# Expert products of an MoE layer in three single-pass parts instead of one float32 product, with the parts made by ScalarE and VectorE

## The chip, the cores and the metric

The kernel runs on one core of a Trainium2 chip. The metric is the device time of one execution in microseconds. The kernel before took 673.37 us, the median of three runs (673.04 to 673.84).

## The reference

One layer of a decoder trunk for 1024 prompt tokens and 64 sample tokens (1088 in all) with 1024 channels: RMSNorm, one input projection to 2048 columns for four token mixers, an output projection with residual, then RMSNorm and a mixture of experts (a group of 8 experts is chosen first, then the best two in it), residual, final RMSNorm. The change touches the experts:

```python
hg = jnp.einsum('nd,edf->nef', xt, w_gate.astype(x.dtype))   # 32 experts, d = 1024, f = 128
hu = jnp.einsum('nd,edf->nef', xt, w_up.astype(x.dtype))
act = jax.nn.silu(hg) * hu * gates[:, :, None]
out = jnp.einsum('nef,efd->nd', act, w_down.astype(x.dtype))
```

Only the two chosen experts of a token have a gate that isn't zero, so the kernel gathers for each expert the rows of its tokens.

## The kernel before

Every engine has its own hand-written program and they meet at semaphores, so the order of the work on an engine is the order of the code. After the projections (up to about 376 us of the span) comes routing: counts, places and a table of the tokens of each expert. Then come the expert blocks. A block is up to 128 rows of one expert; there are 32 blocks, n = 0 to 31, one for each expert, and behind them as many overflow blocks as experts have more than 128 rows. In this run there are three, n = 32 to 34 (35 blocks in all).

For block n the engines do this:

- POOL (GpSimd) issues **gather n**, an indirect DMA of the rows of the normed tokens from DRAM into one of four slots of `xg` (L1047), and later **scatter n**, an indirect DMA of the block's result to DRAM (L1062). In its program gather n+3 stands ahead of scatter n-1. Before the first gather POOL zeroes all four slots with one memset (L1070).
- PE: **T(n)**, 8 transposes of the gathered rows into PSUM (L1918). **GU(n)**, gate and up at once: 8 float32 matmuls with 256 moving columns, of which each shows as two records in the trace (L1932, "x16"). **AT(n)**, one transpose (L1941). **D(n)**, the down projection, 2 float32 matmuls of 512 columns, 4 records (L1952).
- ACT: `hTm`, the copy of T(n) out of PSUM (L862), silu (L869), the copy of AT(n) (L877), half of the output (L886).
- DVE: the product of silu and up, `actv` (L1542), the other half of the output, `outb` (L1550).

The order on PE is T(n+1), AT(n-1), GU(n), D(n-1), and then the same for the next n. Ahead of the blocks DVE computes how many overflow blocks there are (L1515 to L1533).

SP loads the weights of a block: gate, up and down, 512 KB each, 1.57 MB in all (L506). Eight sets fit in SBUF (`wfirst` holds three, `wlater` five), so the load for block n starts once D(n-8) has ended. The loads are held back by a second rule: the up part for block n isn't issued before all three parts of block n-1 have landed:

```python
if m == 1 and not (first and j <= FIRST):
    sp.wait_ge(w_in_sem[(j - AHEAD) % LAP], 48 * (lap(i, j - AHEAD) + 1))
```

So the time at which the up part for n+1 is issued tells when the weights of block n had landed; this time is called **L(n)** below.

The rest of the kernel already works with split values elsewhere: the input projection (L1663, L1709) and the output projection (L1840) take each float32 factor as a high part (a copy rounded to the type float32r, by ACT, L606) and a low part (the difference, by DVE, L1150), and sum three products high·high, high·low, low·high, each one pass through PE.

Of the kernel before, what the change touches and what calls it, by code (L numbers as in the profile page):

```python
# [19 lines left out]
F32 = mybir.dt.float32  # L20
# [96 lines left out]
def build_layer(nc, a):  # L117
    with ExitStack() as ctx:
# [15 lines left out]
        o_end = o_uc + 2 * CL * 4  # L134
# [17 lines left out]

        xg = at("xg", [P, XG, D], o_xg)
# [7 lines left out]
        def opair(i):  # L161
# [44 lines left out]
        otmp = at("otmp", [1, OVER, NE], o_w + 8192)  # L206
        otmp2 = at("otmp2", [1, OVER, NE], o_w + 10240)
# [6 lines left out]
        wsT = sb("wsT", [P, NG, P])  # L214
        wsb = sb("wsb", [NS, NG, NS])
        pw = sb("pw", [P, 2, P])
# [71 lines left out]
            "xt_done", "htm_ready", "gu_done", "sg_ready", "act_ready", "at_done", "att_ready",  # L288
# [285 lines left out]
        def _(act):  # L574
# [280 lines left out]
            def expert_hT(i, j):  # L855
# [6 lines left out]
                nc.scalar.activation(hTm[:, j % 2, :, :], src, ACT.Copy).then_inc(s["htm_ready"], 1)  # L862
# [26 lines left out]
            def step(i, j, first, last):  # L889
                if not last:  # L890
                    expert_hT(i, j + 1)
                else:
                    with act.If(total > 0):
                        expert_hT(i, j + 1)
# [7 lines left out]
            act.wait_ge(s["o_done"], TILES)  # L902
            expert_hT(0, 0)
# [12 lines left out]
            with act.Fori(0, OVER // LAP) as i:  # L916
                with act.If(i * LAP < total):
                    for j in range(LAP):
                        with act.If(i * LAP + j < total):
                            with act.If(i * LAP + j + 1 < total):  # L920
                                expert_hT(i + NE // LAP, j + 1)
                            expert_actT(i + NE // LAP, j - 1)
                            expert_silu(i + NE // LAP, j)
                            expert_out(i + NE // LAP, j - 1)
# [26 lines left out]
        def _(pool):  # L951
# [117 lines left out]
            pool.wait_ge(s["o_done"], TILES)  # L1069
            do(g.memset(xg[:].rearrange("p s d -> p (s d)"), 0.0), s["xg_zero"])  # L1070
# [13 lines left out]
            for b in range(-3, NE + 1):  # L1084
                if b == 0:
                    pool.wait_ge(s["idx_ready"], 2)
                if b + 3 < NE:
                    c = (b + 3) * CAPB
                    gather(b + 3, gidxs[:, c:c + 1], tab[:, c:c + 1], b if b >= 1 else None)
                else:  # L1090
                    if b + 3 == NE:
# [3 lines left out]
                    gather_over(b + 3 - NE)  # L1095
# [9 lines left out]
            def over_from(o):  # L1105
# [3 lines left out]
                with pool.If(total > o):  # L1109
                    if o + 4 < OVER:  # L1110
                        gather_over(o + 4)
# [12 lines left out]
        def _(dve):  # L1124
# [389 lines left out]
            n_e, incl = ov[:, 0, :], ov[:, 1, :]  # L1514
            do(ts(ovi[:], carry[0:1, :], float(P - 1), None, ALU.add))  # L1515
            do(ts(ovi[:], ovi[:], 7, None, ALU.logical_shift_right))
            do(ts(n_e, ovi[:], 1.0, -1.0, ALU.max, ALU.add))
            do(v.tensor_tensor_scan(incl, ones[0:1, 0:NE], n_e, 0.0, ALU.mult, ALU.add))
            grid = [1, OVER, NE]
            for k in range(2):  # L1520
                dve.wait_ge(h2_stored[k], 16 * ((TILES + 1 - k) // 2))
            do(tt(otmp[:], incl.unsqueeze(1).broadcast_to(grid), iob[:].unsqueeze(2).broadcast_to(grid),
                  ALU.is_le))
            do(v.tensor_reduce(ovb[:, 0, :], otmp[:], AX_X, ALU.add))
            do(tt(otmp2[:], otmp[:], n_e.unsqueeze(1).broadcast_to(grid), ALU.mult))
            do(v.tensor_reduce(ovb[:, 1, :], otmp2[:], AX_X, ALU.add))
            do(ts(ovb[:, 0, :], ovb[:, 0, :], float(NE - 1), None, ALU.min))
# [500 lines left out]
```

## Time and profile before

| | |
|---|---|
| median of the runs | 673.37 us (673.04 to 673.84) |
| profiled execution, its own time | 673.23 us |
| its span, first to last instruction | 671.4 us |
| busy in the span: PE, DVE, ACT, POOL | 580.5, 369.5, 204.3, 97.6 us |
| moved by DMA | 116.27 MB, mean 173 GB/s |

The profiled execution's own time is 1.83 us more than its span; that is what lies around the span. PE's busy time counts overlapping records and waits inside them, so it says that PE was always occupied, not that it ran at its peak. The expert blocks take about 399 to 617 us of the span. After them come the pairing of the results, the residual and the last norm, which use no PE.

### The profile page before, as it was taken

The numbers are of one execution on the slowest core, as the hardware profiler recorded it, in microseconds if no ns is written. First come the engines' busy times: TensorE is split into PE (matmuls) and PEld (weight loads), VectorE is DVE, ScalarE is ACT, GpSimd is POOL, SyncE is SP. The second block draws the span as 40 slices with busy tenths as digits, with TensorE's granted clock in tenths as the row PEclk, the third lists the DMA queues.
The fourth block names the chain that finished last, engine by engine and source line by source line (L and its number), as shares of the span: only waits on it lengthen the run. The fifth ranks groups of instructions, "written<-read, shape, count | busy, mean of one in ns | idle before, by whom it ended". The sixth has DMA issues, their size and how long they took to land. (4 is left out here: it accounts for less than half of the span.)

```text
span 671.4 us, 9514 instructions
## 1 busy us (share of the span) xinstructions
PE 580.5 (86%) x3131; PEld 496.4 (74%) x3131; DVE 369.5 (55%) x653; ACT 204.3 (30%) x351; POOL 97.6 (15%) x151
## 2 busy tenths in 40 slices
PE   3899999999999998999999449999999999997000
PEld 2899999988898897888887338777778777774000
DVE  4838997999996966566665841111111111112497
ACT  6732112311324273122121123233333323332132
POOL 4300002000000000000000231332233333322000
PEclk9999999999999999999999759999999999999555
DMA  9660211120122123641220776888989999940784
GB/s 320 133 143 1 63 32 32 53 63 16 48 72 95 33 94 138 238 157 64 95 79 32 255 241 218 297 307 285 317 294 351 367 316 344 322 186 26 288 349 161
DMA packets 51439, 116.27 MB, mean 173 GB/s; under 512 B 8434, under 2 KB 26743, under 8 KB 50295
## 3 DMA queue, kind: packets, MB, share of 16 engines
q1 hardware_dynamic: 42899, 92.82, 40.7%
q0 software_dynamic: 6656, 17.84, 7.6%
q10 hardware_dynamic: 1828, 4.96, 2.0%
q8 instruction: 25, 0.41, 0.3%
q14 instruction: 31, 0.25, 0.1%
HBM read 99.75 MB, written 20.68 MB: 179 GB/s over the span
## 5 line engine op out<-in xcount | busy, mean ns | idle before, releaser
L1663 PE MATMUL ps<-at_hT,at_ring 128*128 128x384 f32 x936 | 165.7, 333 | 1.1 <-ACT at_wk L629 1.1
L1663 PEld LDWEIGHTS ps<-at_hT,at_ring 128*128 128x128 f32 x936 | 155.8, 188 | 6.5 <-issue 5.0
L1840 PE MATMUL ps<-at_hT,at_mring 128*128 128x512 f32 (+1 forms) x432 | 102.6, 393 | 1.9 <-DVE at_mring L1343 1.2
L1840 PEld LDWEIGHTS ps<-at_hT,at_mring 128*128 128x128 f32 (+1 forms) x432 | 77.3, 182 | 21.2 <-DVE at_mring L1343 1.6
L1542 DVE TENSOR_TENSOR at_actv<-at_sg,ps 128x128 f32<-128x128 f32 x35 | 10.1, 287 | 146.2 <-ACT at_sg L869 101.6
L1190 DVE SCALAR_TENSOR_TENSOR at_mixP<-at_uc,sb_par,at_mixP 128x1024 f32<-128x1024 f32 x60 | 77.4, 1289 | 2.1
L1932 PE MATMUL ps<-at_wlater,at_hTm 128*128 128x256 f32 x320 | 72.4, 379 | 0.0
L1932 PEld LDWEIGHTS ps<-at_wlater,at_hTm 128*128 128x128 f32 x320 | 59.2, 190 | 7.2
L1932 PE MATMUL ps<-at_wfirst,at_hTm 128*128 128x256 f32 x240 | 56.3, 389 | 0.0
L1918 PEld LDWEIGHTS ps<-sb_ident,at_xg 128*128 128x128 f32 x280 | 37.7, 193 | 23.6 <-issue 21.8
L1932 PEld LDWEIGHTS ps<-at_wfirst,at_hTm 128*128 128x128 f32 x240 | 45.9, 197 | 6.3 <-issue 0.3
L1550 DVE COPY at_outb<-ps 128x512 f32<-128x512 f32 x35 | 24.2, 692 | 41.5 <-PE ps L1952 41.5
L1062 POOL DMA_INDIRECT scratch_out<-at_outb,at_tab x32 | 30.4, 950 | 102.3 <-DVE at_outb L1550 98.8
L1918 PE MATMUL ps<-sb_ident,at_xg 128*128 128x128 f32 x280 | 38.7, 283 | 7.4 <-DMA at_xg<-scratch_h,at_gidxs 6.2
L581 ACT ACTIVATE at_wk<-at_x 128x1024 f32<-128x1024 f32 (+1 forms) x18 | 19.0, 1058 | 79.9 <-DVE at_x L1415 52.4
L862 ACT ACTIVATE at_hTm<-ps 128x1024 f32<-128x1024 f32 x35 | 35.8, 1024 | 15.7 <-PE ps L1918 15.4
L1619 PE MATMUL ps<-sb_ident,at_wk 128*128 128x128 f32 (+1 forms) x144 | 23.6, 319 | 17.6 <-DVE at_wk L1133 13.9
L1047 POOL DMA_INDIRECT at_xg<-scratch_h,at_gidxs x32 | 31.7, 991 | 47.7 <-issue 36.7
L1952 PE MATMUL ps<-at_wlater,at_actT 128*128 128x512 f32 x80 | 37.6, 592 | 0.0
L886 ACT ACTIVATE at_outb<-ps 128x512 f32<-128x512 f32 x35 | 20.9, 597 | 52.0 <-PE ps L1952 52.0
L1619 PEld LDWEIGHTS ps<-sb_ident,at_wk 128*128 128x128 f32 (+1 forms) x144 | 21.2, 200 | 20.3 <-issue 13.1
L869 ACT ACTIVATE at_sg<-ps 128x128 f32<-128x128 f32 x35 | 9.7, 278 | 84.0 <-PE ps L1932 79.2
(238 smaller groups left out, 656.4 us busy)
## 6 DMA issues: line engine op xcount, KB each, us to landing
at_wlater<-in_expert_w_gate SPq DMA_DIRECT2D x20, 512.0 KB
at_wlater<-in_expert_w_up SPq DMA_DIRECT2D x20, 512.0 KB
at_wlater<-in_expert_w_down SPq DMA_DIRECT2D x20, 512.0 KB
at_raw<-in_w_in SPq DMA_DIRECT2D x16, 512.0 KB, 4.0
at_opair_p<-scratch_out SPq DMA_DIRECT2D x8, 1024.0 KB, 12.0
at_wfirst<-in_expert_w_gate SPq DMA_DIRECT2D x15, 512.0 KB
at_wfirst<-in_expert_w_up SPq DMA_DIRECT2D x15, 512.0 KB
at_wfirst<-in_expert_w_down SPq DMA_DIRECT2D x15, 512.0 KB
```

What stands on the lines that cost most here:

```text
L862: nc.scalar.activation(hTm[:, j % 2, :, :], src, ACT.Copy).then_inc(s["htm_ready"], 1)
L886: nc.scalar.activation(outb[:, j % 2, 0:512], ps[:, 5, :], ACT.Copy)\
L1047: g.indirect_dma_start(xg[0:n, b % XG, :], None, hs, bass.IndirectOffsetOnAxis(ap=index[0:n, :], axis=0), bounds_check=last_token, oob_is_ ...
L1062: g.indirect_dma_start(orow, bass.IndirectOffsetOnAxis(ap=index[0:n, :], axis=0), outb[0:n, b % 2, :], None, bounds_check=last_pair, oob_i ...
L1190: do(stt(y, x, par[:, c, k:k + 1], y, ALU.mult, ALU.add))
L1550: v.tensor_copy(outb[:, j % 2, 512:D], ps[:, 6, :]).then_inc(s["ob_dve"], 1)
L1619: mm = pe.transpose(ps[:, banks + k // 4, k % 4 * P:k % 4 * P + n], wk[0:n, i % 2, 0:D].rearrange("p (q k) -> p k q", k=KC)[:, k, :], iden ...
L1663: mm = pe.matmul(ps[:, bank + r, 0:t1 - t0], w[:, wpart, k * P:(k + 1) * P], hT[:, hpart, k, t0:t1], start=(m, wpart, hpart) == (0, 0, 0), ...
L1840: mm = pe.matmul(ps[0:n, b + r, :], mring[:, 1 - i % 2, mpart, k * P:k * P + n], wo[:, wpart, k, r * 512:(r + 1) * 512], start=(c, mpart, ...
L1918: mm = pe.transpose(ps[:, k // 4, k % 4 * P:(k % 4 + 1) * P], xg[:, j % XG, :].rearrange("p (q k) -> p k q", k=KC)[:, k, :], ident[:])
L1932: mm = pe.matmul(ps[:, 2 + j % 2, 0:2 * FF].rearrange("p (g f) -> p g f", g=2), hTm[:, j % 2, k, :], w[:, :, k, :], start=k == 0, stop=k = ...
L1952: mm = pe.matmul(ps[:, 5 + r, :], actT[:, j % 2, :], wexp(j)[:, q:q + 512], start=True, stop=True)
```

## The change

There are four parts.

1. GU(n) is no longer 8 float32 matmuls but 24 float32r matmuls: high·high, high·low, low·high for each of 8 chunks. The low part of the tokens (`hTm_lo`, L1587 of the changed kernel) is made by DVE from PSUM and `hTm`. The high part of the weights (`whi`, 2 halves, one buffer each, so that the half for n+1 is written once GU(n) has read it) is made by ACT, and the low part (`wlo`) by DVE, which overwrites the landed weights.
2. POOL's order: gather n+4 stands ahead of scatter n-1, where it was gather n+3.
3. The overflow counts on DVE are moved behind the first conversions and cut in two pieces.
4. The four slots of `xg` are zeroed by four ACT copies (three behind the last `square`, one behind the last `h2T` copy) and not by POOL.

Some small arrays also move to other addresses (`wsT`, `wsb`, `pw`), which share room with `hTm_lo`. The core of the diff:

```diff
+        whi = [at("whi0", [P, 2, KC // 2, FF], o_raw + D * 2, F32R),
+               at("whi1", [P, 2, KC // 2, FF], o_sg + D * 4, F32R)]
...
-        hTm = at("hTm", [P, 2, KC, P], o_hTm)
+        hTm = at("hTm", [P, 2, KC, P], o_hTm, F32R)
+        hTm_lo = [at("hTm_lo0", [P, KC, P], o_w + 2 * D * 4, F32R),
+                  at("hTm_lo1", [P, KC, P], o_late, F32R)]
...
+                if i >= LAST:
+
+                    act.wait_ge(s["o_done"], TILES)
+                    for n in range(3) if i == LAST else range(3, XG):
+                        zeros = ones[:].unsqueeze(1).broadcast_to([P, KC, P])
+                        do(A(xg[:, n, :].rearrange("p (k t) -> p k t", k=KC), zeros, ACT.Copy, scale=0.0),
+                           s["xg_zero"])
...
+            def expert_whi(i, j, h):
+
+                b = i * LAP + j
+                act.wait_ge(w_in_sem[j % LAP], 48 * lap(i, j) + 48)
+                if not (isinstance(b, int) and b < 1):
+                    act.wait_ge(s["gu_done" if h else "gu_half"], b)
+                nc.scalar.activation(whi[h][:], half(wexp(j), h), ACT.Copy).then_inc(s[f"w_hi{h}"], 1)
...
             def step(i, j, first, last):
+                ahead(i, j, last, expert_hT)
                 if not first:
                     expert_actT(i, j - 1)
+                ahead(i, j, last, whi0)
                 expert_silu(i, j)
+                ahead(i, j, last, whi1)
                 if not first:
                     expert_out(i, j - 1)
 
 
             act.wait_ge(s["o_done"], TILES)
+            whi1(0, 0)
+            act.wait_ge(s["idx_ready"], 2)
+            whi0(0, 0)
             expert_hT(0, 0)
...
-            pool.wait_ge(s["o_done"], TILES)
-            do(g.memset(xg[:].rearrange("p s d -> p (s d)"), 0.0), s["xg_zero"])
+            pool.wait_ge(s["xg_zero"], XG)
...
-            def step(i, j, first):
+            def expert_hT_lo(i, j):
+
+                b = i * LAP + j
+                dve.wait_ge(s["htm_hi"], b + 1)
+                if not (isinstance(b, int) and b < 2):
+                    dve.wait_ge(s["gu_done"], b - 1)
+                src = ps[:, 0:2, :].rearrange("p b (k t) -> p (b k) t", t=P)
+                v.tensor_tensor(hTm_lo[j % 2][:], src, hTm[:, j % 2, :, :].bitcast(F32),
+                                ALU.subtract).then_inc(s["htm_lo"], 1)
+
+            def expert_wlo(i, j, h):
+
+                b = i * LAP + j
+                dve.wait_ge(s[f"w_hi{h}"], b + 1)
+                v.tensor_tensor(half(wexp_lo(j), h), half(wexp(j), h), whi[h][:].bitcast(F32),
+                                ALU.subtract).then_inc(s[f"w_lo{h}"], 1)
...
+            def step(i, j, first, last):
+                ahead(i, j, last, expert_hT_lo)
+                ahead(i, j, last, wlo0)
                 expert_act(i, j)
+                ahead(i, j, last, wlo1)
                 if not first:
                     expert_out(i, j - 1)
 
...
+            wlo1(0, 0)
+            wlo0(0, 0)
+            expert_hT_lo(0, 0)
+            overflow_counts()
+            expert_hT_lo(0, 1)
+            overflow_blocks()
+            wlo0(0, 1)
+            expert_act(0, 0)
+            wlo1(0, 1)
...
                 if not early(b, 1):
-                    pe.wait_ge(s["htm_ready"], b)
+                    pe.wait_ge(s["htm_lo"], b)
...
-                pe.wait_ge(s["htm_ready"], b + 1)
+                pe.wait_ge(s["htm_lo"], b + 1)
                 if not early(b, 2):
                     pe.wait_ge(s["act_ready"], b - 1)
-                pe.wait_ge(w_in_sem[j % LAP], 48 * lap(i, j) + 48)
-                w = wexp(j)[:, 0:2 * D].rearrange("p (g k f) -> p g k f", g=2, k=KC)
+                out = ps[:, 2 + j % 2, 0:2 * FF].rearrange("p (g f) -> p g f", g=2)
                 for k in range(KC):
-                    mm = pe.matmul(ps[:, 2 + j % 2, 0:2 * FF].rearrange("p (g f) -> p g f", g=2),
-                                   hTm[:, j % 2, k, :], w[:, :, k, :], start=k == 0, stop=k == KC - 1)
-                mm.then_inc(s["gu_done"], 1)
+                    h = k // 4
+                    if k % 4 == 0:
+                        pe.wait_ge(s[f"w_lo{h}"], b + 1)
+                    high, low = whi[h][:, :, k % 4, :], half(wexp_lo(j), h)[:, :, k % 4, :]
+                    x, x_low = hTm[:, j % 2, k, :], hTm_lo[j % 2][:, k, :]
+                    pe.matmul(out, x, high, start=k == 0, stop=False)
+                    pe.matmul(out, x, low, start=False, stop=False)
+                    mm = pe.matmul(out, x_low, high, start=False, stop=k == KC - 1)
+                    if k % 4 == 3:
+                        mm.then_inc(s["gu_done" if h else "gu_half"], 1)
```

On PE, this is the program of the kernel before around GU(1): the transposes T(2), AT(0), GU(1), D(0).

```order
738 L1918 MATMUL ps<-sb_ident,at_xg 128x128 x8
739 L1941 MATMUL ps<-sb_ident,at_actv 128x128
740 L1932 MATMUL ps<-at_wfirst,at_hTm 128x256 x8
741 L1952 MATMUL ps<-at_wfirst,at_actT 128x512 x2
742 L1918 MATMUL ps<-sb_ident,at_xg 128x128 x8
```

In the changed kernel the same place reads as follows (`at_whi_54` is the first half of the high weights, `at_wfirst_lo` the low part in place of the landed weights, `at_hTm_lo_61` the low part of the tokens of block 1).

```order
761 L2024 MATMUL ps<-sb_ident,at_xg 128x128 x8
762 L2053 MATMUL ps<-sb_ident,at_actv 128x128
763 L2042 MATMUL ps<-at_whi_54,at_hTm 128x256
764 L2043 MATMUL ps<-at_wfirst_lo,at_hTm 128x256
765 L2044 MATMUL ps<-at_whi_54,at_hTm_lo_61 128x256
766 L2042 MATMUL ps<-at_whi_54,at_hTm 128x256
767 L2043 MATMUL ps<-at_wfirst_lo,at_hTm 128x256
768 L2044 MATMUL ps<-at_whi_54,at_hTm_lo_61 128x256
```

One row of 8 matmuls has become 24 rows of one, in threes; the order of T, AT, GU, D is the same.

On DVE, this is the end of the overflow counts and the first blocks before (`at_ovt` is the table of overflow blocks).

```order
408 L1532 CAST at_ovt<-at_ovb 1x16
409 L1533 CAST at_ovt<-at_ov 1x1
410 L1542 TENSOR_TENSOR at_actv<-at_sg,ps 128x128 x2
411 L1550 COPY at_outb<-ps 128x512
412 L1542 TENSOR_TENSOR at_actv<-at_sg,ps 128x128
413 L1550 COPY at_outb<-ps 128x512
```

And this is it in the changed kernel, from the last row of the overflow table to the end of the step of block 2 (`at_whi_54` and `at_whi_55` are the two halves).

```order
413 L1644 CAST at_ovt<-at_ov 1x1
414 L1594 TENSOR_TENSOR at_wfirst_lo<-at_wfirst,at_whi_54 128x2x512
415 L1570 TENSOR_TENSOR at_actv<-at_sg,ps 128x128
416 L1594 TENSOR_TENSOR at_wfirst_lo<-at_wfirst,at_whi_55 128x2x512
417 L1587 TENSOR_TENSOR at_hTm_lo_60<-ps,at_hTm 128x1024
418 L1594 TENSOR_TENSOR at_wfirst_lo<-at_wfirst,at_whi_54 128x2x512
419 L1570 TENSOR_TENSOR at_actv<-at_sg,ps 128x128
420 L1594 TENSOR_TENSOR at_wfirst_lo<-at_wfirst,at_whi_55 128x2x512
421 L1578 COPY at_outb<-ps 128x512
422 L1587 TENSOR_TENSOR at_hTm_lo_61<-ps,at_hTm 128x1024
```

Three subtractions of 1024 columns stand around the two instructions that DVE had in a block, and `actv`, for which PE waits, stands behind two of them. On ACT the step changes in the same way. Before, for block 1 and its neighbours:

```order
153 L862 ACTIVATE at_hTm<-ps 128x1024
154 L877 ACTIVATE at_actT<-ps 128x128
155 L869 ACTIVATE at_sg<-ps 128x128
156 L886 ACTIVATE at_outb<-ps 128x512
157 L862 ACTIVATE at_hTm<-ps 128x1024
```

And in the changed kernel:

```order
159 L885 ACTIVATE at_hTm<-ps 128x1024
160 L908 ACTIVATE at_actT<-ps 128x128
161 L893 ACTIVATE at_whi_54<-at_wfirst 128x1024
162 L900 ACTIVATE at_sg<-ps 128x128
163 L893 ACTIVATE at_whi_55<-at_wfirst 128x1024
164 L917 ACTIVATE at_outb<-ps 128x512
165 L885 ACTIVATE at_hTm<-ps 128x1024
```

Silu now stands behind the first half of the next block's weights, and the output half behind the second.

## Rows read from the trace of the kernel before

**Rows 1.** The page: span and instructions.

```profile
span 671.4 us, 9514 instructions
```

**Rows 2.** The chain of work that ended last: start us, us, what.

```profile
389.98 4.42 DMA at_xg<-scratch_h,at_gidxs
...
394.54 1.96 PE ps L1918 x8
...
399.64 5.45 PE ps L1932 x16
...
406.18 3.46 PE ps L1932 x16
...
412.35 3.46 PE ps L1932 x16
...
609.00 3.46 PE ps L1932 x16
...
617.31 0.70 DVE at_outb L1550
```

**Rows 3.** Groups by form, 0 to 400 us: busy us, mean ns of one.

```profile
L1709 PE MATMUL ps<-at_ring,at_hT 128*128 128x256 f32 x192 | 23.2, 283 | 0.0
```

**Rows 4.** Instructions of a line or tile: ns min/median/max, first and last start.

```profile
L1150 DVE TENSOR_TENSOR at_ring<-at_raw,at_ring x16: 1224/1225/1227, 20.5 to 220.0; 128x1024 fp32r<-128x1024 f32 x16
L606 ACT ACTIVATE at_ring<-at_raw x16: 1058/1062/1066, 14.6 to 212.9; 128x1024 fp32r<-128x1024 f32 x16
L1140 DVE TENSOR_TENSOR at_hT<-ps,at_hT x9: 692/1224/1225, 13.5 to 35.4; 128x1024 fp32r<-128x1024 f32 x8, 128x512 fp32r<-128x512 f32 x1
```

**Rows 5.** Groups by form, 400 to 620 us.

```profile
L862 ACT ACTIVATE at_hTm<-ps 128x1024 f32<-128x1024 f32 x34 | 34.8, 1024 | 11.4 <-PE ps L1918 11.1 <-issue 0.3
L1062 POOL DMA_INDIRECT scratch_out<-at_outb,at_tab x32 | 30.4, 950 | 102.3 <-DVE at_outb L1550 98.8 <-issue 3.5
...
L1047 POOL DMA_INDIRECT at_xg<-scratch_h,at_gidxs x28 | 27.3, 975 | 33.4 <-issue 33.4
L1550 DVE COPY at_outb<-ps 128x512 f32<-128x512 f32 x35 | 24.2, 692 | 41.5 <-PE ps L1952 41.5
...
L1542 DVE TENSOR_TENSOR at_actv<-at_sg,ps 128x128 f32<-128x128 f32 x35 | 10.1, 287 | 146.2 <-ACT at_sg L869 101.6 <-issue 44.6
```

**Rows 6.** The timeline between projection and first block: start us, us.

```profile
375.43 3.52 POOL L1070 MEMSET at_xg<- 128x4096 f32 x1 [0.20 <-POOL sb_rs L963]
...
377.90 0.60 ACT L833 ACTIVATE at_h2T<-ps 128x512 f32<-128x512 f32 x1 [3.63 <-issue]
...
390.35 0.20 DVE L1512 TENSOR_TENSOR sb_stage<-sb_stage 128x36 f32<-128x36 f32 x1
...
395.98 0.14 DVE L1533 CAST at_ovt<-at_ov 1x1 int32<-1x1 f32 x1
```

**Rows 7.** What SP's queue waited for, 400 to 600 us, and two of its issues.

```profile
SPq L506 <- DMA at_wlater<-in_expert_w_down: 68.2, 14, 7.0
SPq L506 <- DMA at_wfirst<-in_expert_w_down: 46.5, 11, 7.3
...
419.54 0.33 SPq L506 DMA_DIRECT2D at_wfirst<-in_expert_w_up  x1
...
588.60 0.33 SPq L506 DMA_DIRECT2D at_wfirst<-in_expert_w_up  x1
```

**Rows 8.** Stretches: busy us by engine, granted clock, DMA share, GB/s.

```profile
400.00:405.00 5.00, 5.00 (x17) 4.06 (x16) 0.00 (x0) 1.99 (x2) 0.05 (x1) 0.64 0.97 251
411.54:593.50 181.96, 181.96 (x860) 141.90 (x859) 28.94 (x59) 61.58 (x119) 56.77 (x63) 1.00 0.91 318
499.90:505.32 5.42, 5.42 (x27) 4.15 (x26) 0.98 (x2) 1.33 (x3) 1.41 (x2) 1.00 0.82 287
518.25:526.02 7.77, 7.77 (x38) 6.22 (x37) 0.98 (x2) 2.22 (x5) 2.51 (x3) 1.00 1.03 394
593.00:594.00 1.00, 1.00 (x6) 0.88 (x5) 0.00 (x0) 0.00 (x0) 0.82 (x1) 1.00 0.17 62
```

More of the change, by code:

```diff
@@ L887, in expert_out, with ahead, whi0, whi1 @@
                     .then_inc(s["ob_act"], 1)
-            def step(i, j, first, last):
+            def ahead(i, j, last, work_on):
                 if not last:
-                    expert_hT(i, j + 1)
+                    work_on(i, j + 1)
                 else:
                     with act.If(total > 0):
-                        expert_hT(i, j + 1)
+                        work_on(i, j + 1)
+            def whi0(i, j):
+                expert_whi(i, j, 0)
+            def whi1(i, j):
+                expert_whi(i, j, 1)
+            def step(i, j, first, last):
+                ahead(i, j, last, expert_hT)
                 if not first:
                     expert_actT(i, j - 1)
+                ahead(i, j, last, whi0)
                 expert_silu(i, j)
+                ahead(i, j, last, whi1)
                 if not first:
@@ L922, in _ @@
                             expert_actT(i + NE // LAP, j - 1)
+                            with act.If(i * LAP + j + 1 < total):
+                                whi0(i + NE // LAP, j + 1)
                             expert_silu(i + NE // LAP, j)
+                            with act.If(i * LAP + j + 1 < total):
+                                whi1(i + NE // LAP, j + 1)
                             expert_out(i + NE // LAP, j - 1)
@@ new lines, in expert_wlo, with ahead @@
+            def expert_wlo(i, j, h):
[3 more added lines that the diff above has]
+                                ALU.subtract).then_inc(s[f"w_lo{h}"], 1)
+            def ahead(i, j, last, work_on):
+                if not last:
+                    work_on(i, j + 1)
+                else:
+                    with dve.If(total > 0):
+                        work_on(i, j + 1)
@@ L1553, in step, with wlo0, wlo1 @@
+            def wlo0(i, j):
+                expert_wlo(i, j, 0)
+            def wlo1(i, j):
+                expert_wlo(i, j, 1)
+            def step(i, j, first, last):
+                ahead(i, j, last, expert_hT_lo)
+                ahead(i, j, last, wlo0)
                 expert_act(i, j)
+                ahead(i, j, last, wlo1)
                 if not first:
                     expert_out(i, j - 1)
-            for j in range(LAP):
-                step(0, j, first=j == 0)
-            with dve.Fori(1, NE // LAP) as i:
-                for j in range(LAP):
-                    step(i, j, first=False)
@@ new lines, in _ @@
+            wlo1(0, 0)
[7 more added lines that the diff above has]
+            wlo1(0, 1)
+            for j in range(1, LAP):
+                step(0, j, first=False, last=False)
+            with dve.Fori(1, NE // LAP - 1) as i:
+                for j in range(LAP):
+                    step(i, j, first=False, last=False)
+            total = dve.value_load(ovt[0:1, 2 * OVER:2 * OVER + 1], min_val=0, max_val=OVER)
@@ L1563, in _ @@
+            for j in range(LAP):
+                step(NE // LAP - 1, j, first=False, last=j == LAP - 1)
             with dve.If(total < 1):
```

92 lines of the change are left out of this document (53 added, 39 removed).

## The prediction

> **What bounds the kernel now.** I read the chain of work that ended last first. From the first gather's landing to the end of the last block it is PE work in program order, with a steady step: GU(1) begins at 406.18, GU(2) at 412.35, GU(34) at 609.00, which is 6.17 us a block, of which GU takes 3.46, and the last output is copied at 617.31 [rows 2]. So in this stretch a microsecond off PE's program is a microsecond off the end, for as long as nothing else is late. What else could be late is seen next, in SP's waits: SP waits 68.2 + 46.5 us, 25 times, for weights that have to land before it may issue the next ones [rows 7]. L(8) is 419.54 and L(33) 588.60 [rows 7], 25 loads in 169.06 us, 6.76 us a load. The loads are thus already slower than the blocks, and it isn't seen only because eight sets of weights fit: the lead is being eaten. The stretches show it from the side of the DMA engines: 0.91 share and 318 GB/s over 182 us, 57.9 MB [rows 8]. The reader should see that PE is the bound now and that the DMA side has a small reserve at the end: L(34) is about 594 (the share falls to 0.17 at 593 [rows 8]; I add 1 us until the semaphore), and GU(34) begins at 609.00, 15 us later.
>
> **GU in three products.** The trace has this very form in another place: 192 matmuls of 256 columns on float32r, high·high, high·low, low·high, in 23.2 us, 0.121 us each [rows 3]. 24 of them are 2.90 us where GU took 3.46 [rows 2], 0.56 us less a block and 5.61 us a block instead of 6.17. From GU(1) to GU(34) that is 33 x 0.56 = 18.5 us, and 0.56 more in GU(34) itself: 19.0 us less. The price from below is the width alone (24 x 256 columns at 2.4 GHz, 2.56 us, another 11 us less); from above it is what GU takes now. I take the row, since the order of the operands is the same.
>
> **The conversions in a block.** DVE gets three subtractions of 1024 columns, 1.225 us each, from SBUF or PSUM alike [rows 4], beside `actv` 0.287 and `outb` 0.692 [rows 5]: 4.65 us of 5.61. ACT gets two copies of 1.062 [rows 4] beside `hTm` 1.024 [rows 5] and small ones. Both fit, but the order counts, so I step through a block with GU(n) beginning at 0. It is half done at 1.45: `whi0` for n+1 until 2.5, `wlo0` until 3.8. GU(n) ends at 2.9: silu, then `whi1` until 4.3, `wlo1` until 5.6. `actv` comes behind `wlo0`, at 4.1, and AT(n) needs it at 5.5. GU(n+1) begins at 5.61 and needs `wlo0` (3.8) then and `wlo1` (5.6) at 7.05. T(n+2) ends at 5.5, `hTm` follows until 6.6 and its low part until 7.9, a whole step ahead of GU(n+2). Nothing stands in PE's way, with 1.4 us to spare. The cost is nothing while this reserve holds.
>
> **The start.** T(0) begins at 394.54 and ends 1.96 later [rows 2]. T(1) now waits for the low part of T(0) too, 1.22 us, and GU(0) begins at about 400.9 and not at 399.64. It runs mostly at the lower clock level: the granted clock was 0.64 between 400 and 405, thus 1.2 GHz for most of it [rows 8], and the old GU(0) took 5.45 [rows 2]. 24 matmuls, most at 256 columns by 1.2 GHz, give about 4.6, until 405.5. DVE is later: the overflow counts took from about 390.8 (two small instructions begin at 390.35) to 396.1 [rows 6], 5.3 us, and now stand between the low parts of blocks 0 and 1, so that the second piece ends at about 406, `wlo0` of block 1 at 407.3 and `actv` of block 0 at 407.6. AT(0) waits for it, and GU(1) begins at 407.7, not at 406.18: 1.5 us more.
>
> **Zeros on ACT, gathers sooner.** The memset lasted 3.52 us on POOL, from 375.43 to 378.95 [rows 6], and POOL's next work, the first gather, came at 389.98 [rows 2], so removing it gives nothing. Three copies on ACT (at most 1.06 each) end at about 377.7, and the `h2T` copy behind them began at 377.90 [rows 6]: nothing to 0.5 us. That gather n+4 passes scatter n-1 moves no gather that PE waits for: after block 1 PE waits for no gather in the chain [rows 2]. It gives a block of lead more.
>
> If only these terms counted, the end would come 19.0 - 1.5 = 17.5 us sooner.
>
> **What is late next: the weights.** The bytes don't change, the time for them does. With D(0) about 0.8 us later (412.3), the load for block 8 starts so much later, and SP goes from load to load by landings as now, so that L(34) moves from 594 to 594.8. The gathers and scatters of the same stretch run on the same engines: 57.9 MB less 27 loads of 1.573 MB leaves 15.4 MB for about 29.5 blocks, 0.52 MB each [rows 8]. At L(34) the changed kernel will be some 2.3 blocks further, 1.2 MB more in the same time. What a megabyte beside a load costs I take from two loads: 5.42 us at 287 GB/s and 7.77 us at 394 GB/s [rows 8], 1.51 MB more in 2.35 us, 1.6 us per MB. From below it is nothing (share 0.91, so there are gaps), from above 1 MB at the mean 318 GB/s, 3.1 us. So L(34) = 594.8 + 1.9 = 596.7, between 594 and 599. Without waits GU(34) would begin at 609.00 - 18.5 + 1.5 = 592.0, and needs the weights some 2.8 us before. It waits: from L(34) on, `whi0` 1.06, `wlo0` 1.23, `actv` of the block before 0.29, AT 0.11 and gaps between engines make 2.9 us. GU(34) = 599.6, which is 9.4 sooner than 609.00; its own 0.56 makes 10.0. The waits begin at block 28 or so, and take back 7.5 of the 17.5 us.
>
> The Trainium skill, DMA: Bandwidth & Descriptors, section Where 436 GB/s comes from, puts the limit of transfers between HBM and SBUF at about 358 GB/s a core. By that the 57.9 MB need 162 us, not 182, the weights would be in time and the whole 17.5 us would stay. The trace has a load at 394 GB/s, above it, and a mean of 318, below it [rows 8]; I go by the landings.
>
> **The sum.** 673.23 us of the profiled execution (671.4 of span [rows 1] and 1.83 around it) less 10.0 is 663.2; the median of the runs is 0.14 higher: 663.4 us. What comes after block 34 isn't touched.
>
> **Rivals.**
> - *A, the weights take over at about block 28* (above): 663.4, with its bounds 660.5 to 666. For it speak the 25 waits of SP on landings. Chance 0.57.
> - *B, DMA keeps up*: the gaps at 0.91 share take the extra traffic and the loads themselves go faster when the engines are never left waiting. PE sets the step to the end: 673.4 - 17.5 = 655.9, 654 to 660. Against it: the rule that holds the up part back for the landing leaves gaps that more traffic doesn't shorten. The rule on 358 GB/s above would end here. Chance 0.18.
> - *C, DVE becomes the bound, slower than before*: POOL issues two indirect DMAs a block, 0.95 and 0.975 us [rows 5]. If DVE's subtractions with two SBUF operands stood still for them, DVE would need 4.65 + 1.92 = 6.57 us a block, 0.40 more than PE needs now: 33 x 0.40 + 1.5 = 14.7 us more, 688. It decides from 1.5 us of standstill a block on. For it: only 0.96 us of DVE's step are free. Against: `sb_stage` at 390.35, with two operands in SBUF, ran in 0.20 us [rows 6] while POOL was issuing the gather of 389.98 [rows 2]. Chance 0.08, with other ways to be slower.
> - *D, the loads are hit harder*: each megabyte at 3.1 us, and the wait of ACT for weights ahead of silu delays also the outputs and scatters: 666 to 671. Chance 0.14.
> - *E, it does nothing to the time*, gain and waits equal: 0.03.
>
> The Trainium skill, SBUF — State Buffer, section Who interferes with whom, says that a VectorE instruction with two SBUF inputs contends with a GpSimd instruction that reads SBUF. This is the mechanism of C. The small instruction at 390.35 doesn't show it; no long one beside a gather is in this trace.
>
> **Numbers.** The likeliest is A, 663.4. A and B and the nearer part of D hold 8 in 10: 655 to 668.5. A measurement of this kernel can tell some 0.2% (1.3 us) from no change. Faster 0.88, same 0.03, slower 0.09.
>
> **What would show it.** In the changed profile: the matmuls of GU at 0.121 us each and 5.6 us a block on PE between 420 and 540; GU(1) at 407 to 408; from about 560 on PE idle 1 us a block, with `whi` waiting for the weights' DMA; SP waiting for landings as before and the last up part issued at about 591; DVE's subtractions at 1.225 us. The prediction is wrong if PE never waits after 420 (B), if the subtractions show 1.7 us or more beside POOL's issues (C), or if a load takes over 7 us in the mean (D).

## The result and the profile after

The changed kernel takes **667.98 us** (three runs, 659.28 to 667.98), against 673.37 us before (five runs, 672.87 to 674.35): ratio 0.9876, 95% interval 0.9844 to 0.9908. Of its five runs two are left out of these ranges and the ratio, one of 843.35 us at a mean granted clock of 0.677 (the others had 0.937 to 0.942), and one of 669.70 us, which is no slower than the slowest of the six further runs below. It gained 5.4 us where 10.0 were forecast. The profiled execution took 667.98 us, with a span of 666.1 us, 1.88 us around it.

The chain of work that ended last, columns as in [rows 2], from the first gather to the end of the blocks:

```profile
390.71 4.47 DMA at_xg<-scratch_h,at_gidxs
...
395.31 1.96 PE ps L2024 x8
...
406.67 1.23 DVE at_wfirst_lo L1594
407.89 0.21 DVE at_actv L1570
408.15 0.33 PE ps L2053
...
414.12 6.86 DMA at_wfirst<-in_expert_w_down
...
594.00 7.33 DMA at_wfirst<-in_expert_w_down
...
601.43 1.07 ACT at_whi L893
...
603.68 0.27 DVE at_actv L1570
603.99 0.33 PE ps L2053
604.32 0.22 PE ps L2042
```

In [rows 2] this stretch was PE from beginning to end. Now it leaves PE behind D(0): from 414.12 on it is the landings of weights, each of which releases the next issue on SP, and it returns to PE only at the last block. The end is that of the forecast: landing, `whi`, `actv`, AT(33), GU(34) at 604.32 (599.6 forecast). From the last landing (601.38) to GU(34) it took 2.94 us, 2.9 were forecast.

What SP and ACT waited for (us in total, times, longest), in the order of [rows 7]:

```profile
SPq L522 <- DMA at_wlater<-in_expert_w_down: 88.5, 16, 7.9
SPq L522 <- DMA at_wfirst<-in_expert_w_down: 45.4, 11, 6.2
...
ACT at_whi L893 <- DMA at_wlater<-in_expert_w_down: 17.9, 6, 5.2
ACT at_whi L893 <- DMA at_wfirst<-in_expert_w_down: 11.5, 6, 3.8
```

SP waits for landings as before. New is that ACT waits too: 12 times the weights weren't there when `whi` wanted them. The stretches, columns as in [rows 8]:

```profile
412.96:520.00 107.04, 107.04 (x723) 88.80 (x723) 86.46 (x98) 78.96 (x117) 42.46 (x38) 1.00 0.91 307
420.99:593.56 172.57, 162.82 (x1078) 133.60 (x1077) 128.33 (x146) 115.17 (x174) 66.80 (x63) 1.00 0.92 314
530.00:540.00 10.00, 7.55 (x52) 6.46 (x53) 6.79 (x10) 5.56 (x10) 1.97 (x2) 1.00 0.99 315
560.00:570.00 10.00, 6.91 (x48) 5.71 (x47) 5.20 (x6) 3.74 (x6) 2.48 (x3) 1.00 0.86 295
```

Until 520 PE has no idle time. Between 530 and 540 and between 560 and 570 it is idle for 2.5 and 3.1 us in ten. The second row is from L(8) to L(33): 25 loads in 172.57 us, 6.90 each (6.76 before, [rows 7]), at 314 GB/s, about the rate of [rows 8]. In this execution more work per microsecond did not make the transfers faster.

### The profile page after: what moved, and what is told of

Read it like the earlier page. It is cut to its first block, busy times and chain, and to the rows that moved or that the text cites. A ratio compares the mean times of both kernels' runs of the same rounds, so it can differ in the third digit from the quotient of the medians.

```text
span 666.1 us, 10376 instructions
## 1 busy us (share of the span) xinstructions
PE 561.1 (84%) x3411; PEld 490.0 (74%) x3411; DVE 487.6 (73%) x758; ACT 275.6 (41%) x425; POOL 105.5 (16%) x150
## 4 chain that ended last, share of the span: by engine, by line
PE 29%; DMA 28%; DVE 18%; ACT 3%; issue 2%; SPq 2%; POOL 0%; DVEq 0%; POOLq 0%; ACTq 0%
DMA at_wlater<-in_expert_w_down 15%; PE ps L1946 13%; DMA at_wfirst<-in_expert_w_down 11%; PE ps L1769 8%; DVE at_x L1697 4%; PE ps L1987 2%; DVE at_mixP L1240 2%; DVE at_x L1705 2%; SPq L522 2%; DVE at_hT L1200 1%; PE ps L1725 1%; DVE at_lnsq L1425 1%; PE ps L2064 1%; DMA at_opair_p<-scratch_out 1%; DVE at_ring L1200 1%
## 5 line engine op out<-in xcount | busy, mean ns | idle before, releaser
L2042 PE MATMUL ps<-at_whi,at_hTm 128*128 128x256 f32 x280 | 81.8, 292 | 0.0
L2044 PE MATMUL ps<-at_whi,at_hTm_lo 128*128 128x256 f32 x280 | 79.0, 282 | 0.0
L1594 DVE TENSOR_TENSOR at_wlater_lo<-at_wlater,at_whi 128x1024 fp32r<-128x1024 f32 x40 | 49.0, 1225 | 22.1 <-ACT at_whi L893 14.7
L1587 DVE TENSOR_TENSOR at_hTm_lo<-ps,at_hTm 128x1024 fp32r<-128x1024 f32 x35 | 42.8, 1222 | 16.1 <-ACT at_hTm L885 16.0
L2042 PEld LDWEIGHTS ps<-at_whi,at_hTm 128*128 128x128 f32 x280 | 53.6, 191 | 0.1
L2044 PEld LDWEIGHTS ps<-at_whi,at_hTm_lo 128*128 128x128 f32 x280 | 53.4, 191 | 0.0
L893 ACT ACTIVATE at_whi<-at_wlater 128x1024 fp32r<-128x1024 f32 x40 | 42.2, 1056 | 23.0 <-DMA at_wlater<-in_expert_w_down 17.9
L1594 DVE TENSOR_TENSOR at_wfirst_lo<-at_wfirst,at_whi 128x1024 fp32r<-128x1024 f32 x30 | 36.6, 1224 | 15.8 <-ACT at_whi L893 14.5
L2043 PE MATMUL ps<-at_wlater_lo,at_hTm 128*128 128x256 f32 x160 | 44.9, 280 | 0.0
L885 ACT ACTIVATE at_hTm<-ps 128x1024 fp32r<-128x1024 f32 x35 | 35.9, 1027 | 11.1 <-PE ps L2024 11.0
```

The source lines that it names most:

```text
L893: nc.scalar.activation(whi[h][:], half(wexp(j), h), ACT.Copy).then_inc(s[f"w_hi{h}"], 1)
L1587: v.tensor_tensor(hTm_lo[j % 2][:], src, hTm[:, j % 2, :, :].bitcast(F32), ALU.subtract).then_inc(s["htm_lo"], 1)
L1594: v.tensor_tensor(half(wexp_lo(j), h), half(wexp(j), h), whi[h][:].bitcast(F32), ALU.subtract).then_inc(s[f"w_lo{h}"], 1)
L2042: pe.matmul(out, x, high, start=k == 0, stop=False)
L2043: pe.matmul(out, x, low, start=False, stop=False)
L2044: mm = pe.matmul(out, x_low, high, start=False, stop=k == KC - 1)
```

## The experiments

The expectations give the theories letters. W is the forecast's account: PE is faster until the weights are late, and their landings, held apart by the rule on the up part, then set the end. The others look for the missing gain elsewhere: in what the transfers can carry, in PE's own work, or in the conversions.

**The changed kernel again** (no edit), to see how its time scatters.

> The changed kernel once more, without an edit, to learn how far its runs lie apart. Theory W (the landings of the weights set the end of the blocks): the runs scatter by several us, as the landings do, while the kernel before, whose PE never waits, stays within 1.5 us; median 664 to 669. Rival P (PE's program sets the end and the first result was low or high by chance): scatter as small as that of the kernel before, about 1 us.

Measured: 666.85 us (663.02 to 670.21), ratio 0.9906 (0.9872 to 0.994). The kernel before, run beside it, lay within 3.0 us in 11 runs (1.5 were expected), this one within 7.2 in six. In the profiled one (span 661.9) L(8) was 419.32 and L(33) 586.15, not 593.56: the same loads, the last of them 7.4 us sooner, 6.67 us each where the first profile had 6.90 and the kernel before 6.76. The landings scatter, and since they set the end, so does the time. A difference of 0.1 or 0.2 us a load between two profiles is therefore not by itself an effect of the change.

**The up part waits for the load before the last one.**

```diff
-AHEAD = 1
+AHEAD = 2
```

> The up part for block n waits for the landing of block n-2 and not n-1, so that more of the loads is in flight; nothing else is changed. Theory W with gaps (DMA share 0.92, the rule leaves the engines waiting): the mean load falls from 6.9 us to about 6.3, the waits of ACT for weights vanish or begin after block 30, 656 to 661 us. Rival S (the DMA engines are already full, and their rate is all there is): no change within 1.5 us, 666 to 669, loads still 6.9 us.

Measured: **653.52 us** (652.74 to 654.11), ratio 0.97 (0.9683 to 0.9716), 2.5 us below the range that W gave. SP's waits, then the stretch 420 to 560:

```profile
SPq L522 <- PE ps L2064: 75.3, 20, 14.0
SPq L522 <- DMA at_wlater<-in_expert_w_down: 31.8, 10, 5.3
SPq L522 <- DMA at_wfirst<-in_expert_w_down: 15.6, 4, 6.0
```

```profile
420.00:560.00 140.00, 140.00 (x941) 115.78 (x940) 113.36 (x127) 103.18 (x153) 58.76 (x53) 1.00 1.00 359
```

SP now waits mostly for a free set of weights (PE's D), not for landings. The DMA share is 1.00 at 359 GB/s, where the changed kernel has 0.93 and 318 GB/s between the same times. PE is never idle. The bytes are the same, so what held the weights up was the issue rule, and it cost 13.3 us (against 666.85 beside it; 14.5 against the first result). Gaps between loads are not all of it: while the engines were busy they moved 318/0.93 = 342 GB/s with the old rule and 359 with the new one, and why that rate rose too the runs don't show. PE's program and the conversions are unchanged here and everything fits in PE's step, so neither of them held the changed kernel back, nor did what the DMA engines can carry.

**Fewer bytes, the rule left alone.** From block 8 on only 128 of the 1024 columns of the down part are loaded.

```diff
-                    sp.dma_start(wexp(j)[:, m * D:(m + 1) * D], src)\
+                    n = D if first or m < 2 else P
+                    sp.dma_start(wexp(j)[:, m * D:m * D + n], src[:, 0:n])\
```

> From block 8 on only 128 of the 1024 columns of the down part are loaded (the rest of that buffer keeps the expert of eight blocks before), so a load is 1.11 MB and not 1.57; everything else is issued and computed as in the changed kernel. Theory W: no wait for weights is left, PE sets the step to the end at 5.5 to 5.6 us a block, 655 to 657 us. Rival C (the conversions on ACT and DVE hold PE up too): no faster than 662.

Measured: 653.52 us (653.0 to 653.95), ratio 0.9698 (0.968 to 0.9717), 1.5 us below W's range, PE without idle time between 420 and 560 and the DMA share still 0.91. The same end by another way: with weights in time, PE's program and the start of the blocks alone give 653.5.

**One product of three.**

```diff
-                    pe.matmul(out, x, high, start=k == 0, stop=False)
-                    pe.matmul(out, x, low, start=False, stop=False)
-                    mm = pe.matmul(out, x_low, high, start=False, stop=k == KC - 1)
+                    mm = pe.matmul(out, x, high, start=k == 0, stop=k == KC - 1)
```

> GU keeps only the product high by high, 8 matmuls and not 24; low parts are still made and waited for, so the two low products are left out of the result. PE needs 1.9 us less a block. Theory W: the loads are what they are, the end moves by at most 2.5 us (GU of the last block and the product behind it), 664 to 668 us, and ACT waits for weights from about block 12 on. Rival P: 33 times 1.9 us less, or as far as DVE's 4.65 us a block allow, 635 to 640 us.

Measured: 664.77 us (663.6 to 667.56), ratio 0.9869 (0.9841 to 0.9897), against 666.85 for three products beside it. ACT waited for weights for 49 us (29 in the changed kernel):

```profile
ACT at_whi L893 <- DMA at_wlater<-in_expert_w_down: 35.8, 10, 4.9
ACT at_whi L893 <- DMA at_wfirst<-in_expert_w_down: 13.5, 6, 3.1
```

Two thirds of GU's work gone, 1.9 us a block, and 2 us in all gained: in the kernel as changed, PE's speed is no longer the question.

**The kernel before with AHEAD = 2.**

> The kernel before, with AHEAD = 2 in place of 1 and nothing else: the up part of block n waits for the weights of block n-2. By W (in the changed kernel the landings and the gaps that the rule leaves took 14 us back) nothing changes here, because PE sets the step of the kernel before to the end: 672.0 to 674.8 us, with the weights of the last block there some 35 us ahead instead of 15. If the relaxed rule brought something of its own, for instance a shorter step of PE or less idle at the start, this kernel would gain too: 668 or less. If it does, part of the 20 us of the run with AHEAD = 2 was not a matter of the three products.

Measured: 673.65 us (672.99 to 674.81), ratio 1.0011 (1.0002 to 1.0021). SP waits 122.9 us for PE and 3.7 for landings, and nothing is gained. The looser rule is worth nothing until the three products make PE faster; the three products bring only about a third of their gain until the rule is looser (7.0 of 20.3 us in the runs that stood side by side, 673.80, 666.85 and 653.52).

**Float32 matmuls behind the conversions, AHEAD = 2.**

```diff
-                    pe.matmul(out, x, high, start=k == 0, stop=False)
-                    pe.matmul(out, x, low, start=False, stop=False)
-                    mm = pe.matmul(out, x_low, high, start=False, stop=k == KC - 1)
+                    mm = pe.matmul(out, x.bitcast(F32), high.bitcast(F32), start=k == 0, stop=k == KC - 1)
```

> The changed kernel with AHEAD = 2 and with all conversions on ACT and DVE, their waits and the new order, but GU as 8 float32 matmuls of the tokens' high part with the weights' high part, as long as before (the low parts are made and not read, so the output lacks their products). It prices the conversions and waits by themselves. By the steps of the prediction they are hidden in the steady step (6.17 us a block, PE without waits) and cost 1.5 us at the start: 674 to 676 us. If POOL's or DVE's work beside each other, or the second half of the weights' conversion, cost PE anything in each block, it would be over 680: each 0.2 us a block makes 6.6 us. If the start cost is not there, 673.

Measured: 675.7 us (674.94 to 676.63), ratio 1.004 (1.0025 to 1.0054). Its chain:

```profile
394.80 1.96 PE ps L2024 x8
...
407.97 3.46 PE ps L2042 x16
...
414.15 3.46 PE ps L2042 x16
...
610.80 3.46 PE ps L2042 x16
```

GU(1) to GU(2) is 6.18 us and GU(34) comes 33 blocks later at 6.15 each, as before [rows 2]: in the steady step the conversions cost nothing. From T(0) to GU(1) it takes 13.17 us, where [rows 2] give 11.64: 1.53 us for the start, as forecast. The rest of the 2.4 us is 0.26 us ahead of T(0) and 0.7 behind GU(34).

**One product, AHEAD = 2** (the same edit as above), to see what comes next behind PE.

> The changed kernel with AHEAD = 2 and GU with the high-high product alone, 8 matmuls instead of 24 (the output lacks the two other products). PE then needs 5.53 - 16 x 0.1165 = 3.67 us a block, so what stands next behind PE shows itself. If DVE is next (4.65 us of work a block) and transfers keep up, 34 steps fewer of 0.88 us each than with three products: about 624 us. If transfers are next: with three products and AHEAD = 2 the weights of the last block landed some 20 us ahead, 27 loads in about 163 us, 6.0 us each although they were not held back, so the last block could start some 17 us sooner and no more: 636 us, 630 to 645, with ACT waiting for the weights in the later blocks and the DMA share near 1. With the old rule the same product took 664.8, so under W this run has to be at least 20 us faster than that.

Measured: 649.99 us (648.69 to 651.36), ratio 0.9653 (0.9637 to 0.967). That is 14 us more than the expectation had and outside its range (630 to 645), and only 14.8 less than one product with the old rule, where 20 were the least. The stretch 420 to 560, then the chain from 570 on:

```profile
420.00:560.00 140.00, 114.04 (x547) 75.70 (x546) 111.78 (x131) 98.14 (x156) 61.13 (x53) 0.96 0.99 360
```

```profile
570.06 7.98 DMA scratch_out<-at_outb,at_tab
...
579.80 0.28 ACT at_actT L908
...
580.21 3.60 PE ps L2062 x4
...
589.75 0.74 PE ps L2042 x4
```

The transfers are next, as said: 0.99 share, 360 GB/s with three products as with one, and the last up part at 570.0 us (569.2 with three). But GU(34) then doesn't follow the last weights, and begins no sooner than with three products (about 589 in both). It waits for a scatter of 7.98 us, which must free one of two output buffers before ACT copies half an output, and `actT` and D stand behind that copy. I had counted no such wait. The clock plays a part too: D took 3.60 us there, against 1.72, at a granted clock of 0.57 between 580 and 584 us, after PE had been idle for 4.2 us.

Four runs on one chip follow, the first as the measure for the others.

> The changed kernel with AHEAD = 2, unchanged from the earlier run of it, as the measure for the three runs beside it on the same chip. By W its time scatters little, since PE sets the step to the end: 652.5 to 654.5 us.

Measured: 654.59 us (653.32 to 655.1), ratio 0.9722 (0.9709 to 0.9734).

**Parts 2 and 4 undone, AHEAD = 2.** The memset of POOL is back as well; the core of it is the order of gathers:

```diff
-            for b in range(-XG, NE + 1):
-                n = b + XG
+            for b in range(-3, NE + 1):
+                n = b + 3
...
-                    gather(n, gidxs[:, c:c + 1], tab[:, c:c + 1], b + 1 if b >= 0 else None)
+                    gather(n, gidxs[:, c:c + 1], tab[:, c:c + 1], b if b >= 1 else None)
```

> The changed kernel with AHEAD = 2 and parts 2 and 4 of the change undone: gather n+3 ahead of scatter n-1 as before, and the four slots zeroed by one memset on POOL. The prediction put both parts at nothing (0 to 0.5 us). By W: within 0.5 us of the run with AHEAD = 2 beside it, on either side. If the sooner gathers matter now that PE's step is shorter, PE waits for a gather somewhere and the time is 1 us or more longer. If ACT's zeros delayed the routing, this kernel would be up to 0.5 us faster.

Measured: 668.27 us (666.34 to 670.77), ratio 0.993 (0.9913 to 0.9947), **13.7 us slower** than the run beside it, where 0.5 us on either side were expected: the largest miss of the study. What PE waited for, 400 to 620, and pieces of the chain:

```profile
PE ps L2018 <- DMA at_xg<-scratch_h,at_gidxs: 8.3, 10, 2.0
```

```profile
412.88 0.70 DVE at_outb L1572
...
416.39 7.16 DMA at_xg<-scratch_h,at_gidxs
...
423.69 1.13 PE ps L2018 x8
...
507.86 9.18 DMA at_xg<-scratch_h,at_gidxs
517.18 1.13 PE ps L2018 x8
```

PE's transposes wait for gathers ten times (8.3 us), and their weight loads five times more (7.0 us). The rows say why. In the old order gather n+3 is issued once scatter n-2 has been, and that needs the output of D(n-2); T(n+3) comes two blocks after this D. From `outb` at 412.88 to the landing at 423.55 it is 10.7 us, and `outb` begins 0.7 us behind the end of D(0) at 412.17. These 11.4 us are more than two blocks, which are 11.1 us at 5.53 and were 12.3 at 6.17, and PE waits 0.4 us. When a gather takes 9 us to land beside full DMA engines, it is later still. In the new order three blocks lie between, 16.6 us. Both parts were undone together, so that the loss is the order's is read from these waits and from the start: T(0) began at 394.52 here and at 394.57 in the run beside it, so the zeros made no difference.

**The second piece of the overflow counts in four small ones, AHEAD = 2.**

```diff
-            overflow_blocks()
             wlo0(0, 1)
             expert_act(0, 0)
             wlo1(0, 1)
+            overflow_blocks(0)
             for j in range(1, LAP):
                 step(0, j, first=False, last=False)
+                overflow_blocks(j)
```

> The changed kernel with AHEAD = 2 and the second piece of the overflow counts (2.7 us of DVE work between the low tokens of block 1 and the low weights of block 1) cut into four small pieces that stand at the end of DVE's first four steps. By the prediction's account of the start (DVE is late for AT(0), GU(1) begins at 407.7 and not at 406.2): the low weights of block 1 then come as soon as GU(0) frees them, silu of block 0 as soon as GU(0) ends, and GU(1) begins about 1.1 us sooner: 0.8 to 1.4 us less than the run beside it. If DVE's later steps are delayed by the pieces (0.9 us are free in each), the gain is given back at blocks 2 to 4: no difference.

Measured: 653.41 us (652.64 to 654.03), ratio 0.9706 (0.9693 to 0.9718). The median is 1.2 us below that of the run beside it, but the intervals overlap, and the profiled executions are equally long (spans 651.6 and 651.5). The traces still show a gain, about half of the one expected. From T(0) to D(0) it is 15.51 us here (395.00 to 410.51), and 16.03 in the run beside it (394.57 to 410.60), 16.02 to 16.04 in the other profiles with AHEAD = 2 and in the second one of the changed kernel. The 0.5 us are hidden in the span because T(0) began 0.4 us later, ahead of the edit. In the chain:

```profile
406.32 0.28 ACT at_sg L900
406.59 0.96 ACT at_whi L893
407.57 1.24 DVE at_wfirst_lo L1594
408.85 0.39 PE ps L2047
```

AT(0) does come sooner (406.97, 407.41 beside it), but now the second half of GU(1) waits for its weights, by another way: half of GU(0), `whi0`, silu, `whi1`, `wlo1`. On it stands something that neither the prediction nor this expectation counted. ACT loads a table at silu's line, 1.28 us. In the kernel before that lay in a wait of ACT for GU(0); now it comes only behind `whi0`. The timelines of ACT, before and in this run:

```profile
400.72 1.28 ACT L869 ACT_TABLE_LOAD   x1
405.13 0.28 ACT L869 ACTIVATE at_sg<-ps 128x128 f32<-128x128 f32 x1 [3.13 <-PE ps L1932]
...
405.02 1.28 ACT L900 ACT_TABLE_LOAD   x1
406.32 0.28 ACT L900 ACTIVATE at_sg<-ps 128x128 f32<-128x128 f32 x1
```

GU(0) was done at about 405.4, so silu came some 0.9 us later than it could have. No run takes the load away, so what it costs is an estimate from these rows.

**AHEAD = 3.**

> The changed kernel with AHEAD = 3: the up part waits for the weights of block n-3. With AHEAD = 2 PE never waited for weights and the DMA share was 1.00 at 359 GB/s from 420 to 560 us, so there is nothing left for a still looser rule to give: within 0.7 us of the run with AHEAD = 2 beside it. Slower by 1 us or more would mean that more loads in flight delay the gathers.

Measured: 654.24 us (653.27 to 654.85), ratio 0.9718 (0.9705 to 0.973); share 1.00 at 364 GB/s, no difference.

**Part 2 alone undone, AHEAD = 1.** The same edit of the order in the kernel as changed.

> The changed kernel (AHEAD = 1) with part 2 alone undone: gather n+3 ahead of scatter n-1, as before. With AHEAD = 2 and parts 2 and 4 undone PE waited ten times for a gather (7 to 9 us each to land, the DMA share at 1.00) and the time was 13.7 us longer, against the prediction's nothing. The question is whether that term was also wrong in the kernel as changed, where the share is 0.93. Theory 1, the weights' landings set the end there and late gathers are covered by them: 663 to 670 us, as the changed kernel itself (667.98 and 666.85 in its two sets of runs), with a few waits of PE for gathers. Theory 2, late gathers hold PE, and through D(n-8) the loads too, and the two delays add: 671 to 676 us. In the trace the waits of PE's transposes for gathers tell it, and whether SP waits for landings (theory 1) or for PE (theory 2).

Measured: 670.71 us (668.1 to 677.11), ratio 0.9946 (0.9929 to 0.9964), against 0.9876 and 0.9906 for the changed kernel. In the profiled run, the slowest of the seven:

```profile
PE ps L2024 <- DMA at_xg<-scratch_h,at_gidxs: 10.6, 12, 1.8
...
PE ps L2024 <- DMA at_xg<-scratch_h,at_gcol: 2.0, 2, 1.3
...
SPq L522 <- DMA at_wlater<-in_expert_w_down: 87.7, 16, 8.1
SPq L522 <- DMA at_wfirst<-in_expert_w_down: 54.1, 11, 7.1
SPq L522 <- PE ps L2064: 14.2, 3, 8.5
```

Both waits are there: 14 of PE for gathers, and SP's for landings, which set the chain to the last block (theory 1). Yet the median, between the ranges of both theories, is 2.7 and 3.9 us above those of the changed kernel, measured on other chips, so a part of the late gathers' cost seems to reach the end after all. How, the runs don't settle. The profiled execution says little about it, since 1.2 us of its length have another source: between 409 and 412 us the granted clock was 0.55 (1.00 in the run with AHEAD = 2), and from T(0) to D(0) it took 17.3 us, not 16.0.

## Why the prediction was right, and where it was off

- **The mechanism held.** Rival A: PE gains, then the weights take over. The waits began near 530 us, about block 22, and not at block 28. The experiments agree: weights in time, by another rule or by fewer bytes, and 13 us more come out; less work on PE, and next to nothing does.
- **The number held only narrowly.** The medians, 667.98 and 666.85, lie above A's own bounds (660.5 to 666) and 0.5 us and more inside the whole range to 668.5. The waits took back 14.5 us (13.3 beside the second set) where the forecast had 7.5: PE's gain was larger by 2.8 us and the landings 4.6 us later.
- **GU in three products, -19.0: slightly too small.** In the steady step a matmul took 0.118 us and not 0.121, and with AHEAD = 2 a block took 5.53 us, not 5.61. That is 2.6 us more over 33 blocks. It was of no use in the changed kernel, and it is why AHEAD = 2 gained 20 us where rival B had 17.5. The rows of the input projection were a good price; that other work in them made the difference is a guess.
- **Conversions hidden: right.** The subtractions took 1.21 to 1.24 us each; with the old matmul behind them nothing was lost in the step.
- **The start, +1.5: right in size, half right in cause.** 1.53 us by the float32 run, and from T(0) to GU(1) the changed kernel takes the same 13.17 us. But the counts on DVE were only part of it: with them out of the way 0.5 us came back of the 1.1 expected, and then ACT's way stands there, with a table load of 1.28 us that the prediction's step did not have. GU(0) itself took about 4.4 us in the changed kernel, close to the 4.6 of the forecast.
- **Zeros on ACT, 0 to 0.5: not seen.** The first three zeros end at 378.26, and `h2T` begins at 378.62 after waiting for PE.
- **Gathers one block sooner, 0: wrong.** I argued from the trace of before, in which PE never waits for a gather. But the cover there was two blocks of 6.17 us, and the change itself shortens it, while fuller DMA engines make the gathers slower. The order is worth 13.7 us once the weights are in time, and perhaps 3 to 4 in the kernel as changed, where the runs stood on different chips.
- **L(34) = 596.7: mis-sized, it was 601.3.** This term holds the whole error of 4.6 us. 0.8 us of it came in ahead of T(0), which began at 395.31 and not at 394.54; that is scatter, as the runs with AHEAD = 2, which have the same code up to there, begin it at 394.48 and 394.57. The rest is 27 loads of 6.95 us on average instead of the 6.8 that the forecast came to, some 0.14 us each. I had priced only the additional bytes, with the gaps as they were. The same kernel's next profile had L(33) 7.4 us sooner, and its runs reach from 659.28 to 670.21: 663.4 lies inside them, below the medians. How near the number came is therefore in part luck, and the 0.14 us a load has no cause that the runs show. I hadn't seen this scatter coming: in the kernel before nothing depended on the landings, and its runs lay within 1.5 and 3.0 us.
- **The limit of 358 GB/s.** The Trainium skill, DMA: Bandwidth & Descriptors, section Where 436 GB/s comes from, gives it for transfers between HBM and SBUF. I set it aside because one load ran at 394 GB/s [rows 8]. Over 140 us with the engines' share at 0.99 to 1.00 the changed kernel with AHEAD = 2 or 3 shows 359, 360 and 364 GB/s, near the figure as a mean, and 20 us in the run with parts 2 and 4 undone show 382. That it is this limit that binds them no run shows; the kernel before with AHEAD = 2 moved 336 at a share of 0.98. In the changed kernel it would have been wrong all the same, as the rate there was 318 with the share at 0.93. A figure for what the transfers can do is not one for what this issue rule lets them do.
- **Rivals.** B is what the kernel would have been with AHEAD = 2. C failed. D's bound of 666 to 671 holds the measured median, but by slow loads as such and not by its price per megabyte, and its sign, over 7 us a load, was not reached (6.90). E didn't happen.

## What to carry to other kernels

When the engine that bounds a stretch gets faster, look for the queue that was already slower than it and lived on its lead. Here 6.76 us a load beside 6.17 us a block said it all, and the remedy (letting the next transfer start before the last one has landed) brought nothing to the old kernel and 13 us to the new one. Cover counted in blocks has to be counted again in microseconds with the new step, for every transfer, before any moved issue is priced at nothing. And where two ways are late at the same place, taking one away shows only what lies between them, which is small enough to vanish in the scatter of the whole: compare the stretch that the edit touches, from its own start.

## What was not expected of the hardware

POOL's part of a gather, 975 ns in the mean before [rows 5], got longer beside the subtractions of DVE, which kept their 1.225 us. The same group after, between 400 and 620 us:

```profile
L1097 POOL DMA_INDIRECT at_xg<-scratch_h,at_gidxs x28 | 34.1, 1218 | 32.6 <-issue 31.4 <-PE ps L2024 1.2
```

With AHEAD = 2 it was 1317 ns, in the float32 run 1613 ns. It isn't the load on the DMA engines: the kernel before with AHEAD = 2 kept 975 ns at a share of 0.98. Nor is it the new order, as with the old one and AHEAD = 2 it was 1317 ns too. The scatters stayed at 949 to 981 ns in all of them. Single gathers of the changed kernel tell more:

```profile
510.56 1.23 DVE L1594 TENSOR_TENSOR at_wlater_lo<-at_wlater,at_whi 128x1024 fp32r<-128x1024 f32 x1 [0.37 <-ACT at_whi L893]
511.04 1.65 POOL L1097 DMA_INDIRECT at_xg<-scratch_h,at_gidxs  x1 [0.87 <-issue]
...
549.34 1.04 POOL L1097 DMA_INDIRECT at_xg<-scratch_h,at_gidxs  x1 [0.81 <-issue]
549.39 1.23 DVE L1594 TENSOR_TENSOR at_wfirst_lo<-at_wfirst,at_whi 128x1024 fp32r<-128x1024 f32 x1 [1.53 <-ACT at_whi L893]
...
580.81 1.22 DVE L1587 TENSOR_TENSOR at_hTm_lo<-ps,at_hTm 128x1024 fp32r<-128x1024 f32 x1
581.40 0.94 POOL L1097 DMA_INDIRECT at_xg<-scratch_h,at_gcol  x1 [2.51 <-issue]
```

The first begins while `wlo`, whose two inputs lie in SBUF, has 0.75 us to run, and takes 1.65 us. The second begins just ahead of such a subtraction, the third inside that of the tokens, which has one input in PSUM, and both keep about their time. In the float32 run the rule is plain: each of the 26 gathers from 417 to 572 us begins inside a `wlo`, and ends 0.79 to 0.91 us behind the end of it.

The Trainium skill, SBUF — State Buffer, section Who interferes with whom, says that a VectorE instruction with two SBUF inputs contends with a GpSimd instruction that reads SBUF. That fits, with POOL as the side that pays. But the same section tells of a probe in which `tensor_tensor`, the kind of instruction that `wlo` is, did not stall DMA. Here the subtraction that began first keeps its time and the gather ends behind it, so much the rows show; through what they meet is not shown. In the kernel as changed the wait costs nothing that the chain shows, since POOL is free for half of each block. With the old order and AHEAD = 2 the issue of the gathers stands in the chain, and there it counts. Rival C named the two instructions that meet, and took the wrong one for the victim.
